# The last two layers' projections: where the second half of the rows is transposed

## The chip, the cores and the metric

The kernel runs on one core of one Trainium2 chip. The metric is the device time of one execution in microseconds (us); less is better. The kernel before took 3390.11 us in the median of three runs (3384.37 to 3390.66).

## The reference

The program is a network of four layers on 1024 tokens of width 1024, all in float32. The change touches only the last two, which `second_block` of the reference computes. Each begins in this way:

```
for l in range(DEPTH):                                  # DEPTH = 2
    shift, scale, gate = jnp.split(c_act @ ada_w[l] + ada_b[l], 3, axis=-1)
    h = rms_norm(x, norm_w[l]) * (1.0 + scale[:, None, :]) + shift[:, None, :]
    proj = h @ w_in[l]                                  # [1024, 1024] @ [1024, 2736]
```

Three mixers (a retention, a latent attention and a gated linear attention) work on `proj`, and an output product with a residual ends the layer.

## The kernel before, in words

`second_layer` calls `project` with `front=ModulatedFront(...)`. The front makes `h` in transposed form, the features on the partitions, and cuts it into two parts: `s_x_high` is the value rounded to the fast matmul type (fp32r) and `s_x_low` the rest. The weights are cut in the same manner. Each product is then three passes of eight matmuls (one for each 128 features): high weights by high rows, low weights by high rows, high weights by low rows.

The rows are 8 token tiles of 128. A half is four of them (512 tokens, one PSUM bank wide), KT = 8 is the number of 128-wide feature blocks. In `ModulatedFront` (L2767):

- `scale_rows` (L2813) multiplies a half's rows with their reciprocal root mean square, even tiles on DVE (VectorE), odd ones on ACT (ScalarE).
- `turn` (L2783) transposes on PE (TensorE): a group of four 128x128 transposes fills one bank with one feature block of one half. There are 16 groups, 64 transposes (L2792). Half 0 goes to banks 0 to 7, and half 1 goes to the same banks as half 0 leaves them.
- `modulate` on ACT (L2827) and `modulate_some` on DVE (L2833, blocks 2 and 5 of half 0) apply scale and shift and empty a bank into `s_xT`.
- `take_highs` and `leave_lows` on DVE make `s_x_high` (helper line L167) and `s_x_low` (L172).

Every engine runs its instructions in the order in which the code writes them, and semaphores tie the engines together. In `project`, `first_tiles` (L256) treats the first four jobs (token tiles 0 to 3 by the first 512 columns of weights, banks 0 to 3) together: one pass for all four (L265), then the second (L269), then the third (L273), 32 matmuls each. The later jobs come one at a time (L300, L304, L306). Job 4 writes bank 0 again, so before its first matmul PE waits until job 0 has been copied out of that bank. That copy is DVE's (`empty`, parity 0, helper line L156), and it stands in DVE's program behind everything that the front gives to DVE, `leave_lows` of half 1 the last of it.

The first of the two layers finds its first weights in SBUF already (`prefetched`). The second one loads them when the stage begins. In the rows, the first of these layers works on a tile named `x`, the second on `s_x`; both write `s_xT`, `s_x_high` and `s_x_low`.

Of the kernel before, what the change touches and what calls it, by code (L numbers as in the profile page):

```python
# [15 lines left out]
P = 128  # L16
# [169 lines left out]
def project(nc, core, chunks, slots, x, lows=None, highs=None, beside=None, front=None, ahead=0, modulation=None, prefetched=None):  # L186
# [12 lines left out]
    with stage(nc, "weights_loaded0", "weights_loaded1", "products_ready", "even_emptied", "odd_emptied",  # L199
# [35 lines left out]
        @block.tensor  # L235
        def _(pe):
            if front:
                front.turn(pe, s)
            def first_chunk():


                dst = [core.bank[n][0:jobs[n][1][1][0], 0:jobs[n][1][1][1]] for n in range(int(ends[0]))]
                parts = [[jobs[n][1][0](slot(0, w), part) for w, part in ((highs, x.high), (lows, x.high), (highs, x.low))] for n in range(int(ends[0]))]
                for k in range(KT):
                    pe.wait_ge(s["first_high"], k + 1)
                    pe.wait_ge(s["x_high"], k + 1)
                    for n in range(int(ends[0])):
                        pe.matmul(dst[n], *parts[n][0][k], start=(k == 0), stop=False)
                    pe.wait_ge(s["first_low"], k + 1)
                    pe.wait_ge(s["x_low"], k + 1)  # L250
                    for n in range(int(ends[0])):
                        pe.matmul(dst[n], *parts[n][1][k], start=False, stop=False)
                        mm = pe.matmul(dst[n], *parts[n][2][k], start=False, stop=(k == KT - 1))
                        if k == KT - 1:
                            mm.then_inc(s["products_ready"], 1)

            def first_tiles():


                firsts = [(core.bank[n][0:jobs[n][1][1][0], 0:jobs[n][1][1][1]], jobs[n][1][0]) for n in range(front.FIRST)]  # L260
                pe.wait_ge(s["w_high"], 1)
                for n, (dst, pairs) in enumerate(firsts):
                    front.ready(pe, s, n)
                    for m, (lhsT, rhs) in enumerate(pairs(slot(0, highs), x.high)):
                        pe.matmul(dst, lhsT, rhs, start=(m == 0), stop=False)  # L265
                pe.wait_ge(s["w_low"], 1)
                for dst, pairs in firsts:
                    for lhsT, rhs in pairs(slot(0, lows), x.high):
                        pe.matmul(dst, lhsT, rhs, start=False, stop=False)  # L269
                pe.wait_ge(s["x_low"], KT)  # L270
                for dst, pairs in firsts:
                    for m, (lhsT, rhs) in enumerate(pairs(slot(0, highs), x.low)):
                        mm = pe.matmul(dst, lhsT, rhs, start=False, stop=(m == KT - 1))  # L273
                    mm.then_inc(s["products_ready"], 1)

            if by_depth:
                first_chunk()
            if front:
                first_tiles()
            for n, (c, (pairs, shape, _)) in enumerate(jobs):  # L280
                if by_depth and c == 0 or front and n < front.FIRST:
                    continue
                if front:
                    front.ready(pe, s, n)
                dst = core.bank[n % banks][0:shape[0], 0:shape[1]]
                if n >= banks:

                    pe.wait_ge(emptied[(n - banks) % 2], (n - banks) // 2 + 1)
                if highs is None:
                    if n == starts[c]:  # L290
                        pe.wait_ge(loaded[c % 2], 16 * (c // 2 + 1))
                    ops = pairs(slot(c), x)
                    for m, (lhsT, rhs) in enumerate(ops):
                        mm = pe.matmul(dst, lhsT, rhs, start=(m == 0), stop=(m == len(ops) - 1))
                else:
                    if n == starts[c]:
                        pe.wait_ge(s["w_high"], c if by_depth else c + 1)
                    ops = pairs(slot(c, highs), x.high)
                    for m, (lhsT, rhs) in enumerate(ops):
                        pe.matmul(dst, lhsT, rhs, start=(m == 0), stop=False)  # L300
                    if n == starts[c]:
                        pe.wait_ge(s["w_low"], c if by_depth else c + 1)
                    for lhsT, rhs in pairs(slot(c, lows), x.high):
                        pe.matmul(dst, lhsT, rhs, start=False, stop=False)  # L304
                    for m, (lhsT, rhs) in enumerate(pairs(slot(c, highs), x.low)):
                        mm = pe.matmul(dst, lhsT, rhs, start=False, stop=(m == len(ops) - 1))  # L306
                mm.then_inc(s["products_ready"], 1)
                if modulation:
                    modulation.add_up(pe, s, n)
                if beside and beside.USES_TENSOR:  # L310
                    beside.tensor(pe, s, n)
# [17 lines left out]
        def _(dve):  # L329
# [15 lines left out]
            if front:  # L345
                front.scale_rows(dve, s, 0)
                if prefetched:
                    dve.wait_ge(loaded[0], 16)
                    take_high(dve, slot(0, highs), slot(0)).then_inc(s["w_high"], 1)
                front.scale_rows(dve, s, 1)  # L350
                front.modulate_some(dve, s)
            if by_depth:
                raw, high, low = slot(0), slot(0, highs), slot(0, lows)
                dve.wait_ge(loaded[0], 16)
                for k in range(KT):
                    take_high(dve, high[:, k, :], raw[:, k, :]).then_inc(s["first_high"], 1)
                    dve.wait_ge(s["first_high"], k + 1)
                    leave_low(dve, low[:, k, :], raw[:, k, :], high[:, k, :]).then_inc(s["first_low"], 1)
                    dve.wait_ge(s["x_high"], k + 1)
                    leave_low(dve, x.low[k], x.whole[k], x.high[k]).then_inc(s["x_low"], 1)  # L360
                split_weights(1)
            elif front:
                if not prefetched:
                    dve.wait_ge(loaded[0], 16)
                    take_high(dve, slot(0, highs), slot(0)).then_inc(s["w_high"], 1)
                front.take_highs(dve, s, 0)
                dve.wait_ge(s["w_high"], 1)
                leave_low(dve, slot(0, lows), slot(0), slot(0, highs)).then_inc(s["w_low"], 1)
                front.leave_lows(dve, s, 0)
                front.take_highs(dve, s, 1)  # L370
                front.leave_lows(dve, s, 1)
            else:
                split_weights(0)
# [2393 lines left out]
class ModulatedFront:  # L2767
# [12 lines left out]
        self.x = Halves(*[[HalfTile(halves, k) for k in range(KT)] for halves in (self.whole, self.low, self.high)])  # L2780
        self.x.split = True

    def turn(self, pe, s):  # L2783
        for n in range(2 * KT):
            half, k = divmod(n, KT)
            if k == 0:
                pe.wait_ge(s["scaled_dve"], 2 * half + 2)
                pe.wait_ge(s["scaled_act"], 2 * half + 2)
            if half:
                self.modulated(pe, s, k)  # L2790
            for i in range(4):
                mm = pe.transpose(self.core.bank[k][:, i * P:(i + 1) * P], self.rows[:, 4 * half + i, k * P:(k + 1) * P], self.core.c["ident"])  # L2792
            mm.then_inc(s["rows_turned"], 1)

    def ready(self, pe, s, n):

        if n < BANKS:
            self.modulated(pe, s, KT + n)
        if n in (0, self.FIRST):
            pe.wait_ge(s["x_high"], KT * (1 + n // self.FIRST))  # L2800
        if n == self.FIRST:
            pe.wait_ge(s["x_low"], 2 * KT)

    def modulated(self, eng, s, n):

# [12 lines left out]
            copy_out(eng, self.rows[:, t, :], self.rows[:, t, :], self.core.rstd[:, t:t + 1]).then_inc(s["scaled_act" if on_act else "scaled_dve"], 1)  # L2818

    def modulate(self, act, s):  # L2820
        self.scale_rows(act, s, 0)
        self.scale_rows(act, s, 1)
        for n in range(2 * KT):
            half, k = divmod(n, KT)
            if half or k not in self.BY_DVE:
                act.wait_ge(s["rows_turned"], n + 1)
                act.activation(self.whole[:, half, k, :], self.core.bank[k], ACT.Identity, scale=self.mod.scale[:, k:k + 1],  # L2827
                               bias=self.mod.shift[:, k:k + 1]).then_inc(s["whole_act"], 1)

    def modulate_some(self, dve, s):  # L2830
        for k in self.BY_DVE:
            dve.wait_ge(s["rows_turned"], k + 1)
            dve.tensor_scalar(self.whole[:, 0, k, :], self.core.bank[k], self.mod.scale[:, k:k + 1], self.mod.shift[:, k:k + 1],  # L2833
                              ALU.mult, ALU.add).then_inc(s["whole_dve"], 1)

    def take_highs(self, dve, s, half):
# [1250 lines left out]
```

## Time and profile before

| | us |
|---|---|
| median of three runs | 3390.11 (3384.37 to 3390.66) |
| the profiled execution | 3383.96 |
| its span in the profile | 3382.3 |
| PE busy | 3178.3 (94% of the span) |
| DVE busy | 1891.2 (56%) |
| ACT busy | 1348.8 (40%) |

The span is the profiled time from the first to the last instruction; 1.7 us of the execution lie around it. PE's records are pipelined: a matmul's record begins before that of the one ahead has ended, so the pace of a run of matmuls is read from the distance of starts, not from the duration of one. The stages of the two layers that the change touches begin at about 2170 us and 2772 us of the span. PE's granted clock is given as a share: 1.00 is its full and 0.50 its half rate.

### The profile page before, as it was taken

Reading aid. Unit: us, or ns where it says so; the run is one execution under the profiler, and the core shown is the slowest. Engines: PE = TensorE matmul, PEld = TensorE weight load, DVE = VectorE, ACT = ScalarE, POOL = GpSimd, SP = SyncE. Lnnn points to the kernel's source line nnn. Section 1 sums busy time; section 2 is a strip of 40 time slices with the busy share of each in tenths; the row PEclk is TensorE's granted clock in tenths of the full one; section 3 lists DMA queues with packets and bytes.
Section 4 is the critical chain, followed back from the end, with each engine's and each line's share of the span. In section 5 each row is a group of like instructions: output and inputs, shape, how many; then the busy total and the mean of one; then the engine's idle time right before and its main releaser. Section 6 shows DMA issues by size and latency. Waiting matters only on the chain. (4 is left out here: it accounts for less than half of the span.)

```text
span 3382.3 us, 50928 instructions
## 1 busy us (share of the span) xinstructions
PE 3178.3 (94%) x19709; PEld 2529.0 (75%) x19709; DVE 1891.2 (56%) x3524; ACT 1348.8 (40%) x2487; POOL 397.1 (12%) x313
## 2 busy tenths in 40 slices
PE   7998988899999989979799999899999989999999
PEld 6895567788876867767588888488855678896567
DVE  4535755756747644684756556634366543535654
ACT  2005851656643024552356556511344420134442
POOL 0100020334330000010024324100000000000000
PEclk9999999899999989989899999999999999999999
DMA  7517332868957410012458757610000220100012
GB/s 221 175 58 213 98 113 99 317 269 326 389 214 241 144 40 1 1 63 88 194 228 332 309 212 310 238 33 26 26 17 1 106 101 22 38 26 17 1 67 96
DMA packets 193079, 462.50 MB, mean 137 GB/s; under 512 B 44163, under 2 KB 119255, under 8 KB 184153
## 3 DMA queue, kind: packets, MB, share of 16 engines
q1 hardware_dynamic: 174425, 392.35, 32.2%
q0 software_dynamic: 18432, 67.12, 5.2%
q8 instruction: 148, 2.42, 0.3%
q14 instruction: 74, 0.61, 0.1%
HBM read 383.38 MB, written 73.33 MB: 135 GB/s over the span
## 5 line engine op out<-in xcount | busy, mean ns | idle before, releaser
L1811 PE MATMUL psum<-high_in,e_rowsT_high 128*128 128x256 f32 (+1 forms) x1080 | 330.1, 324 | 5.4 <-DVE e_rowsT_low L172 5.4
L1812 PE MATMUL psum<-high_in,e_rowsT_low 128*128 128x256 f32 (+1 forms) x1080 | 326.3, 320 | 0.0
L172 POOL TENSOR_TENSOR low_down<-w_down,high_out 128x1024 fp32r<-128x1024 f32 x64 | 209.9, 3297 | 295.0 <-ACT high_out L1889 295.0
L1811 PEld LDWEIGHTS psum<-high_in,e_rowsT_high 128*128 128x128 f32 x1080 | 206.5, 191 | 22.3 <-issue 6.1
L1812 PEld LDWEIGHTS psum<-high_in,e_rowsT_low 128*128 128x128 f32 x1080 | 206.8, 192 | 16.2
L3735 DVE CUSTOM_DVE_ANT_0 mla_probs<-psum,mla_mask 128x512 f32<-128x512 f32 (+2 forms) x192 | 97.0, 554 | 100.4 <-PE psum L3602 100.2
L172 DVE TENSOR_TENSOR low_gate<-w_gate,high_in 128x1024 fp32r<-128x1024 f32 x128 | 148.0, 1217 | 7.6 <-ACT high_in L1889 6.6
L172 DVE TENSOR_TENSOR low_up<-w_up,high_in 128x1024 fp32r<-128x1024 f32 x128 | 147.9, 1216 | 0.0
L1816 PE MATMUL psum<-low_up,e_rowsT_high 128*128 128x256 f32 x720 | 130.5, 283 | 0.0
L1889 ACT ACTIVATE high_in<-w_gate 128x1024 fp32r<-128x1024 f32 x128 | 124.8, 1058 | 6.2 <-issue 6.2
L1889 ACT ACTIVATE high_out<-w_down 128x1024 fp32r<-128x1024 f32 x128 | 124.7, 1049 | 3.8 <-DMA w_down<-in_exp_w_down 3.7
L1889 ACT ACTIVATE high_in<-w_up 128x1024 fp32r<-128x1024 f32 x128 | 124.6, 1051 | 0.0
L154 ACT ACTIVATE proj<-psum 128x512 f32<-128x512 f32 (+2 forms) x32 | 16.9, 528 | 259.0 <-PE psum L306 220.2
L156 DVE COPY proj<-psum 128x512 f32<-128x512 f32 (+2 forms) x32 | 19.3, 603 | 174.2 <-PE psum L306 173.6
L3776 ACT ACTIVATE mla_probs<-mla_probs,mla_low 128x256 f32<-128x256 f32 (+7 forms) x128 | 97.9, 767 | 46.5 <-DVE mla_low L3739 45.3
L1897 ACT ACTIVATE e_hiddenT_high<-psum 128x256 fp32r<-128x256 f32 x90 | 34.6, 385 | 204.6 <-PE psum L1825 204.6
L1835 PE MATMUL psum<-high_out,e_hiddenT_high 128*128 128x512 f32 x360 | 115.4, 402 | 0.0
L300 PE MATMUL psum<-ring_high,s_x_high 128*128 128x512 f32 (+3 forms) x576 | 112.9, 338 | 0.0
L1838 PE MATMUL psum<-low_down,e_hiddenT_high 128*128 128x512 f32 x360 | 111.8, 392 | 0.0
L1841 PE MATMUL psum<-high_out,e_hiddenT_low 128*128 128x512 f32 x360 | 111.0, 389 | 0.0
L304 PE MATMUL psum<-ring_low,s_x_high 128*128 128x512 f32 (+3 forms) x576 | 110.6, 334 | 0.0
L306 PE MATMUL psum<-ring_high,s_x_low 128*128 128x512 f32 (+3 forms) x576 | 110.6, 334 | 0.0
(604 smaller groups left out, 7586.1 us busy)
## 6 DMA issues: line engine op xcount, KB each, us to landing
w_gate<-in_exp_w_gate SPq DMA_DIRECT2D x32, 2048.0 KB, 8.8
w_up<-in_exp_w_up SPq DMA_DIRECT2D x32, 2048.0 KB, 13.6
w_down<-in_exp_w_down SPq DMA_DIRECT2D x32, 2048.0 KB, 20.1
ada<-in_ada_w SPq DMA_DIRECT2D x24, 1024.0 KB, 7.5
expert_rows<-e_out POOLq DMA_DIRECT2D x47, 512.0 KB, 7.1
expert_rows<-zero_row SPq DMA_DIRECT2D x33, 512.0 KB, 7.1
token_rows<-x SPq DMA_DIRECT2D x32, 512.0 KB, 2.6
x<-token_rows SPq DMA_DIRECT2D x24, 512.0 KB, 7.2
```

What stands on the lines that cost most here:

```text
L172: return eng.tensor_tensor(low, whole, high, ALU.subtract)
L300: pe.matmul(dst, lhsT, rhs, start=(m == 0), stop=False)
L304: pe.matmul(dst, lhsT, rhs, start=False, stop=False)
L306: mm = pe.matmul(dst, lhsT, rhs, start=False, stop=(m == len(ops) - 1))
L1811: pe.matmul(dst, rows_high[:, k, :], w_high[:, k, cols], start=(k == 0), stop=False)
L1812: pe.matmul(dst, rows_low[:, k, :], w_high[:, k, cols], start=False, stop=False)
L1816: mm = pe.matmul(dst, rows_high[:, k, :], w_low[:, k, cols], start=False, stop=(k == KT - 1))
L1835: pe.matmul(dst, hid_high[:, k, :], w_high[:, k, cols], start=(k == 0), stop=False)
L1838: pe.matmul(dst, hid_high[:, k, :], w_low[:, k, cols], start=False, stop=False)
L1841: mm = pe.matmul(dst, hid_low[:, k, :], w_high[:, k, cols], start=False, stop=(k == HT - 1))
L1889: act.activation(high(e, j)[:, k:k + STEP[j], :], W[e % 2][j][:, k:k + STEP[j], :], ACT.Copy).then_inc(s["w_high_ready"], 1)
L3776: act.activation(row, row, ACT.Exp, bias=low[:, n, side:side + 1], scale=-1.0, accum_out=sums[:, p, i // 4, side, i % 4:i % 4 + 1]).then_i ...
```

## The change

On PE, `turn` now takes a half and a range of feature blocks. Half 0 is transposed ahead, as before. Half 1 is transposed in two pieces of four groups (16 transposes each), one between the first and the second pass of the first four jobs, one between the second and the third, and both use banks 4 to 7. The first pass no longer waits until all of half 0's high parts are there: job 0's matmul m waits for high part m. Job 4 waits for half 1's high parts ahead of its first matmul and for half 1's low parts ahead of its third pass only. On ACT, the scaling of half 1's rows moves behind the modulation of half 0. On DVE, the scaling of half 1's rows moves behind half 0's `take_highs`.

```
--- before.py
+++ after.py
@@ -235,7 +235,7 @@
         @block.tensor
         def _(pe):
             if front:
-                front.turn(pe, s)
+                front.turn(pe, s, 0, range(KT))
             def first_chunk():
 
 
@@ -260,13 +260,17 @@
                 firsts = [(core.bank[n][0:jobs[n][1][1][0], 0:jobs[n][1][1][1]], jobs[n][1][0]) for n in range(front.FIRST)]
                 pe.wait_ge(s["w_high"], 1)
                 for n, (dst, pairs) in enumerate(firsts):
-                    front.ready(pe, s, n)
+                    front.modulated(pe, s, n)
                     for m, (lhsT, rhs) in enumerate(pairs(slot(0, highs), x.high)):
+                        if n == 0:
+                            pe.wait_ge(s["x_high"], m + 1)
                         pe.matmul(dst, lhsT, rhs, start=(m == 0), stop=False)
+                front.turn(pe, s, 1, range(KT // 2))
                 pe.wait_ge(s["w_low"], 1)
                 for dst, pairs in firsts:
                     for lhsT, rhs in pairs(slot(0, lows), x.high):
                         pe.matmul(dst, lhsT, rhs, start=False, stop=False)
+                front.turn(pe, s, 1, range(KT // 2, KT))
                 pe.wait_ge(s["x_low"], KT)
                 for dst, pairs in firsts:
                     for m, (lhsT, rhs) in enumerate(pairs(slot(0, highs), x.low)):
@@ -280,8 +284,8 @@
             for n, (c, (pairs, shape, _)) in enumerate(jobs):
                 if by_depth and c == 0 or front and n < front.FIRST:
                     continue
-                if front:
-                    front.ready(pe, s, n)
+                if front and n == front.FIRST:
+                    pe.wait_ge(s["x_high"], 2 * KT)
                 dst = core.bank[n % banks][0:shape[0], 0:shape[1]]
                 if n >= banks:
 
@@ -302,6 +306,8 @@
                         pe.wait_ge(s["w_low"], c if by_depth else c + 1)
                     for lhsT, rhs in pairs(slot(c, lows), x.high):
                         pe.matmul(dst, lhsT, rhs, start=False, stop=False)
+                    if front and n == front.FIRST:
+                        pe.wait_ge(s["x_low"], 2 * KT)
                     for m, (lhsT, rhs) in enumerate(pairs(slot(c, highs), x.low)):
                         mm = pe.matmul(dst, lhsT, rhs, start=False, stop=(m == len(ops) - 1))
                 mm.then_inc(s["products_ready"], 1)
@@ -347,7 +353,6 @@
                 if prefetched:
                     dve.wait_ge(loaded[0], 16)
                     take_high(dve, slot(0, highs), slot(0)).then_inc(s["w_high"], 1)
-                front.scale_rows(dve, s, 1)
                 front.modulate_some(dve, s)
             if by_depth:
                 raw, high, low = slot(0), slot(0, highs), slot(0, lows)
@@ -364,6 +369,7 @@
                     dve.wait_ge(loaded[0], 16)
                     take_high(dve, slot(0, highs), slot(0)).then_inc(s["w_high"], 1)
                 front.take_highs(dve, s, 0)
+                front.scale_rows(dve, s, 1)
                 dve.wait_ge(s["w_high"], 1)
                 leave_low(dve, slot(0, lows), slot(0), slot(0, highs)).then_inc(s["w_low"], 1)
                 front.leave_lows(dve, s, 0)
@@ -2780,26 +2786,18 @@
         self.x = Halves(*[[HalfTile(halves, k) for k in range(KT)] for halves in (self.whole, self.low, self.high)])
         self.x.split = True
 
-    def turn(self, pe, s):
-        for n in range(2 * KT):
-            half, k = divmod(n, KT)
-            if k == 0:
-                pe.wait_ge(s["scaled_dve"], 2 * half + 2)
-                pe.wait_ge(s["scaled_act"], 2 * half + 2)
+    def bank(self, half, k):
+        return self.core.bank[KT // 2 + k % (KT // 2) if half else k]
+
+    def turn(self, pe, s, half, features):
+        pe.wait_ge(s["scaled_dve"], 2 * half + 2)
+        pe.wait_ge(s["scaled_act"], 2 * half + 2)
+        for k in features:
             if half:
-                self.modulated(pe, s, k)
+                self.modulated(pe, s, KT // 2 + k)
             for i in range(4):
-                mm = pe.transpose(self.core.bank[k][:, i * P:(i + 1) * P], self.rows[:, 4 * half + i, k * P:(k + 1) * P], self.core.c["ident"])
+                mm = pe.transpose(self.bank(half, k)[:, i * P:(i + 1) * P], self.rows[:, 4 * half + i, k * P:(k + 1) * P], self.core.c["ident"])
             mm.then_inc(s["rows_turned"], 1)
-
-    def ready(self, pe, s, n):
-
-        if n < BANKS:
-            self.modulated(pe, s, KT + n)
-        if n in (0, self.FIRST):
-            pe.wait_ge(s["x_high"], KT * (1 + n // self.FIRST))
-        if n == self.FIRST:
-            pe.wait_ge(s["x_low"], 2 * KT)
 
     def modulated(self, eng, s, n):
 
@@ -2818,19 +2816,19 @@
             copy_out(eng, self.rows[:, t, :], self.rows[:, t, :], self.core.rstd[:, t:t + 1]).then_inc(s["scaled_act" if on_act else "scaled_dve"], 1)
 
     def modulate(self, act, s):
-        self.scale_rows(act, s, 0)
-        self.scale_rows(act, s, 1)
         for n in range(2 * KT):
             half, k = divmod(n, KT)
+            if k == 0:
+                self.scale_rows(act, s, half)
             if half or k not in self.BY_DVE:
                 act.wait_ge(s["rows_turned"], n + 1)
-                act.activation(self.whole[:, half, k, :], self.core.bank[k], ACT.Identity, scale=self.mod.scale[:, k:k + 1],
+                act.activation(self.whole[:, half, k, :], self.bank(half, k), ACT.Identity, scale=self.mod.scale[:, k:k + 1],
                                bias=self.mod.shift[:, k:k + 1]).then_inc(s["whole_act"], 1)
 
     def modulate_some(self, dve, s):
         for k in self.BY_DVE:
             dve.wait_ge(s["rows_turned"], k + 1)
-            dve.tensor_scalar(self.whole[:, 0, k, :], self.core.bank[k], self.mod.scale[:, k:k + 1], self.mod.shift[:, k:k + 1],
+            dve.tensor_scalar(self.whole[:, 0, k, :], self.bank(0, k), self.mod.scale[:, k:k + 1], self.mod.shift[:, k:k + 1],
                               ALU.mult, ALU.add).then_inc(s["whole_dve"], 1)
 
     def take_highs(self, dve, s, half):
```

On PE, at the start of the first of the two layers (`consts_49` is the identity matrix, `x_77` the rows), this stood before:

```order
L2792 MATMUL psum<-consts_49,x_77 128x128 x64
L265 MATMUL psum<-ring_high_25761,s_x_high_25752 128x512 x32
L269 MATMUL psum<-ring_low_25760,s_x_high_25752 128x512 x32
L273 MATMUL psum<-ring_high_25761,s_x_low_25751 128x512 x32
L300 MATMUL psum<-ring_high_25761,s_x_high_25752 128x512 x8
```

And this stands there now:

```order
L2799 MATMUL psum<-consts_49,x_77 128x128 x32
L267 MATMUL psum<-ring_high_25761,s_x_high_25752 128x512 x32
L2799 MATMUL psum<-consts_49,x_77 128x128 x16
L272 MATMUL psum<-ring_low_25760,s_x_high_25752 128x512 x32
L2799 MATMUL psum<-consts_49,x_77 128x128 x16
L277 MATMUL psum<-ring_high_25761,s_x_low_25751 128x512 x32
L304 MATMUL psum<-ring_high_25761,s_x_high_25752 128x512 x8
```

The number of transposes and of matmuls is the same; half of the transposes now stand between the passes. The second layer's order is the same.

On DVE, at the same place (`ring` is the weights, `proj` what is copied out of PSUM), this stood before:

```order
L157 TENSOR_SCALAR x_77<-x_77,rstd_56 128x1024 x2
L167 CAST ring_high_25761<-ring_19043 128x4096
L157 TENSOR_SCALAR x_77<-x_77,rstd_56 128x1024 x2
L2833 TENSOR_SCALAR s_xT_25750<-psum,mod_cols_60 128x512 x2
L167 CAST s_x_high_25752<-s_xT_25750 128x512 x8
L172 TENSOR_TENSOR ring_low_25760<-ring_19043,ring_high_25761 128x4096
L172 TENSOR_TENSOR s_x_low_25751<-s_xT_25750,s_x_high_25752 128x512 x8
L167 CAST s_x_high_25752<-s_xT_25750 128x512 x8
L172 TENSOR_TENSOR s_x_low_25751<-s_xT_25750,s_x_high_25752 128x512 x8
L156 COPY proj_321_25753<-psum 128x512
```

And this stands there now:

```order
L157 TENSOR_SCALAR x_77<-x_77,rstd_56 128x1024 x2
L167 CAST ring_high_25761<-ring_19043 128x4096
L2831 TENSOR_SCALAR s_xT_25750<-psum,mod_cols_60 128x512 x2
L167 CAST s_x_high_25752<-s_xT_25750 128x512 x8
L157 TENSOR_SCALAR x_77<-x_77,rstd_56 128x1024 x2
L172 TENSOR_TENSOR ring_low_25760<-ring_19043,ring_high_25761 128x4096
L172 TENSOR_TENSOR s_x_low_25751<-s_xT_25750,s_x_high_25752 128x512 x8
L167 CAST s_x_high_25752<-s_xT_25750 128x512 x8
L172 TENSOR_TENSOR s_x_low_25751<-s_xT_25750,s_x_high_25752 128x512 x8
L156 COPY proj_321_25753<-psum 128x512
```

Only the second pair of row scalings has moved. The last three lines are the same, but the second group of casts (half 1's high parts) waits for half 1's last transposes, which PE now makes between its passes.

## Rows read from the trace of the kernel before

**Rows 1.** The page's first line
```profile
span 3382.3 us, 50928 instructions
```

**Rows 2.** Timeline, PE, first layer's start. Start, us, engine, line, operation, [idle before <- releaser]
```profile
2172.74 9.67 PE L2792 MATMUL psum<-consts,x 128*128 128x128 f32 x64 [12.89 <-ACT x L154]
2182.17 7.51 PE L265 MATMUL psum<-ring_high,s_x_high 128*128 128x512 f32 x32
...
2196.77 7.42 PE L273 MATMUL psum<-ring_high,s_x_low 128*128 128x512 f32 x32
2204.03 1.98 PE L300 MATMUL psum<-ring_high,s_x_high 128*128 128x512 f32 x8
```

**Rows 3.** Timeline, PE, second layer's start
```profile
2775.01 8.93 PE L2792 MATMUL psum<-consts,s_x 128*128 128x128 f32 x64 [7.82 <-ACT s_x L154]
2785.80 7.53 PE L265 MATMUL psum<-ring_high,s_x_high 128*128 128x512 f32 x32 [1.86 <-DVE s_x_high L167]
...
2807.68 1.98 PE L300 MATMUL psum<-ring_high,s_x_high 128*128 128x512 f32 x8
```

**Rows 4.** Busy time of PE in the projections behind job 3, both layers
```profile
2204.00:2449.00 245.00, 244.09 (x1466) 1.00 0.10 29
2808.00:3053.00 245.00, 244.09 (x1466) 1.00 0.10 29
```

**Rows 5.** Timeline, DVE, first layer's start
```profile
2173.97 1.41 DVE L157 TENSOR_SCALAR x<-x,rstd 128x1024 f32<-128x1024 f32 x2
...
2178.09 0.81 DVE L2833 TENSOR_SCALAR s_xT<-psum,mod_cols 128x512 f32<-128x512 f32 x1 [1.71 <-PE psum L2792]
2178.96 2.77 DVE L167 CAST s_x_high<-s_xT 128x512 fp32r<-128x512 f32 x8
2181.65 4.41 DVE L172 TENSOR_TENSOR ring_low<-ring,ring_high 128x4096 fp32r<-128x4096 f32 x1
...
2193.49 4.90 DVE L172 TENSOR_TENSOR s_x_low<-s_xT,s_x_high 128x512 fp32r<-128x512 f32 x8
2198.79 0.69 DVE L156 COPY proj<-psum 128x512 f32<-128x512 f32 x1 [0.40 <-PE psum L273]
```

**Rows 6.** Timeline, DVE, second layer's start
```profile
2780.68 2.29 DVE L167 CAST ring_high<-ring 128x4096 fp32r<-128x4096 f32 x1 [0.26 <-DMA ring<-in_w_in]
2782.89 2.76 DVE L167 CAST s_x_high<-s_xT 128x512 fp32r<-128x512 f32 x8
```

**Rows 7.** Timeline, ACT, first layer's start
```profile
2170.41 4.27 ACT L154 ACTIVATE x<-x,rstd 128x1024 f32<-128x1024 f32 x4 [2.29 <-PEq L84]
...
2178.52 6.81 ACT L2827 ACTIVATE s_xT<-psum,mod_cols 128x512 f32<-128x512 f32 x10 [0.47 <-PE psum L2792]
```

**Rows 8.** Timeline, PE, transposes alone: a window at half clock, one at full clock
```profile
2172.74 4.93 PE L2792 MATMUL psum<-consts,x 128*128 128x128 f32 x22 [12.89 <-ACT x L154]
2177.67 4.63 PE L2792 MATMUL psum<-consts,x 128*128 128x128 f32 x40
```

**Rows 9.** PE by windows, second layer: window, us, busy (records), granted clock, DMA share, GB/s
```profile
2778.00:2779.00 1.00, 1.00 (x9) 0.69 1.04 403
```

**Rows 10.** Timeline, PE: first instruction behind three idle times elsewhere
```profile
361.22 0.66 PE L773 MATMUL psum<-consts,na_probs 128*128 128x128 f32 x4 [2.64 <-DVE na_probs L841]
575.54 1.72 PE L1263 MATMUL psum<-consts,x 128*128 128x128 f32 x14 [2.06 <-DVE xT L1317]
2454.11 3.43 PE L3249 MATMUL psum<-consts,proj 128*128 128x128 f32 x16 [2.31 <-PEq L84]
```

**Rows 11.** PE by windows behind those idle times: granted clock is the fourth number
```profile
362.00:363.00 1.00, 1.00 (x12) 0.50 1.05 246
365.00:366.00 1.00, 1.00 (x11) 0.81 0.74 170
576.00:577.00 1.00, 1.00 (x12) 1.00 0.90 369
2455.00:2456.00 1.00, 1.00 (x6) 0.50 0.86 83
```

More of the change, by code:

```diff
@@ L237, in _ @@
             if front:
-                front.turn(pe, s)
+                front.turn(pe, s, 0, range(KT))
             def first_chunk():
@@ L262, in first_tiles @@
                 for n, (dst, pairs) in enumerate(firsts):
-                    front.ready(pe, s, n)
+                    front.modulated(pe, s, n)
                     for m, (lhsT, rhs) in enumerate(pairs(slot(0, highs), x.high)):
+                        if n == 0:
+                            pe.wait_ge(s["x_high"], m + 1)
                         pe.matmul(dst, lhsT, rhs, start=(m == 0), stop=False)
+                front.turn(pe, s, 1, range(KT // 2))
                 pe.wait_ge(s["w_low"], 1)
@@ L269, in first_tiles @@
                         pe.matmul(dst, lhsT, rhs, start=False, stop=False)
+                front.turn(pe, s, 1, range(KT // 2, KT))
                 pe.wait_ge(s["x_low"], KT)
@@ L282, in _ @@
                     continue
-                if front:
-                    front.ready(pe, s, n)
+                if front and n == front.FIRST:
+                    pe.wait_ge(s["x_high"], 2 * KT)
                 dst = core.bank[n % banks][0:shape[0], 0:shape[1]]
@@ L304, in _ @@
                         pe.matmul(dst, lhsT, rhs, start=False, stop=False)
+                    if front and n == front.FIRST:
+                        pe.wait_ge(s["x_low"], 2 * KT)
                     for m, (lhsT, rhs) in enumerate(pairs(slot(c, highs), x.low)):
@@ L349, in _ @@
                     take_high(dve, slot(0, highs), slot(0)).then_inc(s["w_high"], 1)
-                front.scale_rows(dve, s, 1)
                 front.modulate_some(dve, s)
@@ L366, in _ @@
                 front.take_highs(dve, s, 0)
+                front.scale_rows(dve, s, 1)
                 dve.wait_ge(s["w_high"], 1)
@@ L2781, in __init__, with bank, turn @@
         self.x.split = True
[L2783 to L2788, printed above, removed]
+    def bank(self, half, k):
+        return self.core.bank[KT // 2 + k % (KT // 2) if half else k]
+    def turn(self, pe, s, half, features):
+        pe.wait_ge(s["scaled_dve"], 2 * half + 2)
+        pe.wait_ge(s["scaled_act"], 2 * half + 2)
+        for k in features:
             if half:
-                self.modulated(pe, s, k)
+                self.modulated(pe, s, KT // 2 + k)
             for i in range(4):
-                mm = pe.transpose(self.core.bank[k][:, i * P:(i + 1) * P], self.rows[:, 4 * half + i, k * P:(k + 1) * P], self.core.c["ident"])
+                mm = pe.transpose(self.bank(half, k)[:, i * P:(i + 1) * P], self.rows[:, 4 * half + i, k * P:(k + 1) * P], self.core.c["ident"])
             mm.then_inc(s["rows_turned"], 1)
[L2795 to L2802, printed above, removed]
     def modulated(self, eng, s, n):
@@ L2820, in modulate @@
     def modulate(self, act, s):
-        self.scale_rows(act, s, 0)
-        self.scale_rows(act, s, 1)
         for n in range(2 * KT):
             half, k = divmod(n, KT)
+            if k == 0:
+                self.scale_rows(act, s, half)
             if half or k not in self.BY_DVE:
                 act.wait_ge(s["rows_turned"], n + 1)
-                act.activation(self.whole[:, half, k, :], self.core.bank[k], ACT.Identity, scale=self.mod.scale[:, k:k + 1],
+                act.activation(self.whole[:, half, k, :], self.bank(half, k), ACT.Identity, scale=self.mod.scale[:, k:k + 1],
                                bias=self.mod.shift[:, k:k + 1]).then_inc(s["whole_act"], 1)
@@ L2832, in modulate_some @@
             dve.wait_ge(s["rows_turned"], k + 1)
-            dve.tensor_scalar(self.whole[:, 0, k, :], self.core.bank[k], self.mod.scale[:, k:k + 1], self.mod.shift[:, k:k + 1],
+            dve.tensor_scalar(self.whole[:, 0, k, :], self.bank(0, k), self.mod.scale[:, k:k + 1], self.mod.shift[:, k:k + 1],
                               ALU.mult, ALU.add).then_inc(s["whole_dve"], 1)
```

## The prediction

> **What bounds the kernel now.** I first read the page's span, 3382.3 us [rows 1]; the execution took 3383.96, so 1.7 us lie around it. Then the busy time of the stretches that follow the changed place. From job 4 on, PE is busy 244.09 of 245.00 us in both layers [rows 4]. So PE sets the pace of the projections behind the first four jobs, and whatever moves the start of job 4 moves all that follows by the same amount. The question is only when job 4 starts: at 2204.03 us in the first layer [rows 2] and at 2807.68 in the second [rows 3].
>
> The reader should see how tight the first layer's start already is. PE makes 64 transposes from 2172.74, goes over to the first pass at 2182.17 and runs through to job 4 without a gap [rows 2]. Nothing there waits, so a new order can only gain if it takes work off PE, and this one takes none. In the second layer PE idles once, 1.86 us ahead of the first pass, for the high parts of the rows [rows 3]. They are late because the weights land late: DVE casts the weights at 2780.68, when their transfer has arrived, and only then the rows, at 2782.89 [rows 6].
>
> **Paces.** A pass of 32 matmuls takes 2204.03 - 2196.77 = 7.26 us, 0.227 each [rows 2]. The first layer's transposes run at half clock until about 2177.67 (23 of them in 4.93 us, 0.214 each), and the other 41 take 4.50 us up to 2182.17, 0.11 each [rows 2, 8]. Sixteen at full clock cost 1.76 us. DVE's casts of the rows' blocks follow each other every (2181.65 - 2178.96)/8 = 0.336 us, and one takes 2.77 - 7 x 0.336 = 0.42 [rows 5].
>
> **First layer, step by step.** The first eight groups of transposes don't change, nor does the clock under them. ACT starts to modulate some 2.1 us sooner, since two of its four scalings (4.27/4 = 1.07 us each) move behind it [rows 7]. But DVE casts in order, and ahead of its first cast stands its own block 5, which waits for the sixth group of transposes until 2178.09 and ends at 2178.90 [rows 5]. So the first cast stays at 2178.96: "modulated sooner" buys nothing here.
>
> What changes is that PE need not wait for 64 transposes. Its first matmul starts when the first cast has ended, 2178.96 + 0.42 + 0.05 = 2179.43. Job 0's eight matmuls come at the casts' pace (7 x 0.336 = 2.35), and the other 24 and the slot of the last at 0.227 (25 x 0.227 = 5.68), so the first pass ends at 2187.46. Before it ended at 2182.17 + 7.26 = 2189.43: 2.0 us gained. Then 1.76 us of transposes (2189.22), the second pass (2196.48), 1.76 again (2198.24), and the third pass to 2205.50. PE by itself is now 1.5 us later than 2204.03. The two pieces of transposes (3.5 us) used to stand ahead of the first pass, and only 2.0 us of them are covered by starting sooner: the rest is the idle time while DVE makes the first high part (0.7 us) and the slower eight matmuls.
>
> The second pass needs the low weights. DVE's row scaling (1.41) and the low weights (4.41) follow the casts: 2181.65 + 1.4 + 4.4 = 2187.5, before 2189.22 [rows 5]. No wait. ACT's modulations of half 1 are spread over two pieces and come at 0.67 us each (6.81/10) [rows 7], faster than DVE needs them. A cost of changing between the two kinds of matmul isn't seen at 2182.17, where one follows the other without a gap [rows 2]; the second run is 0.09 us longer than the third (7.51 against 7.42). Four more changes in a layer cost between 0 and 0.4 us; I take 0.
>
> Now DVE's queue, which decides. Half 1's casts wait for the last transposes, which PE now makes at 2198.24 and which DVE sees some 0.2 us later. Then come eight casts (2.69), eight low parts (4.90), and only behind them the copy of job 0 out of bank 0 (0.69) [rows 5]. That is 2198.44 + 2.69 + 4.90 + 0.69 = 2206.72. Job 4 writes that bank, so it starts at 2206.7, not at 2205.5. Before, DVE had ended its low parts at 2198.39 and idled 0.40 us for job 0 [rows 5]: a wait that didn't exist takes the place. First layer: +2.7 us.
>
> **Second layer.** The first cast stays at 2782.89, since the weights' transfer sets it [rows 6]. First matmul 2783.36, end of the first pass 8.03 later at 2791.39 (before 2793.06), then 1.76, 7.26, 1.76: last transposes at 2802.17, third pass over at 2809.43. DVE: 2802.37 + 2.69 + 4.90 + 0.69 = 2810.65, against 2807.68 before: +3.0 us. Here the half 1 transposes had been wholly hidden behind the weights' transfer, and now they aren't.
>
> **The clock in the second layer.** PE's clock rises at about 2778.62 (0.69 over that microsecond) [rows 9]. So 3.6 us at 0.214 are 17 transposes, the other 15 of half 0 end at 2780.3, and PE then idles until 2783.36, 3.0 us, where it idled 1.86. Elsewhere idle times of 2.64 and 2.31 us were followed by half clock, one of 2.06 was not [rows 10, 11]. So I take it that the clock falls. The low spell behind the 2.64 us gap is over during the microsecond from 365, some 3.4 us after 362 [rows 11]. At half clock a matmul takes 2 x 0.227 = 0.45. In 3.4 us PE then does 7.5 of them; at full clock it would do the eight paced ones in 2.4 us and four more in the last 1.0. That is about 4.7 matmuls, 1.1 us. The ends are 0 (no fall) and 3.4 us (two such spells, all of it on unpaced work). I take 1.1.
> The Trainium skill ("TensorE: Matmul & The Clock Gate", "Why this matters for your kernels") asks for no idle gaps above about 3 us between bursts. By that rule the new gap is just at the limit and the fall could stay away, which is the second case below; this case's trace is stricter, with falls behind 2.31 and 2.64 us.
>
> **Sum.** 2.7 + 3.0 + 1.1 = 6.8 us. On the profiled execution that is 3383.96 + 6.8 = 3390.8; on the median 3390.11 + 6.8 = 3396.9. The four times of before lie in two groups (3384.0 and 3384.4, 3390.1 and 3390.7), so the new median may be drawn from either. I say 3396.
>
> **Rivals.**
> - *The clock holds.* Then +5.7 us, 3395.8. For it: the 2.06 us gap that held; against it: 3.0 us is longer than two gaps that didn't.
> - *A long low spell.* The clock stays low over two spells: 5.7 + 3.4 = 9.1 us, 3399.2. For it: the first eight matmuls are spaced at 0.336 us, sparser than any pass of before, and could keep the clock low. Against it: the low spell behind the 2.64 us gap ended within 4 us [rows 11].
> - *The copy isn't waited for.* If the low parts of half 1 overlapped the third pass more than I count, only PE's own 1.5 + 1.8 us would remain: +3.3 us, 3393.4. Against it: DVE's 8.3 us of queue behind the last transpose are longer than the third pass's 7.26.
> - *Not slower: the transposes between the passes are free.* If PE took them in beside the matmuls of the passes (their weights load while a matmul runs), the last transposes and DVE's queue move up by 3.5 us in each layer, to 2203.2 and 2807.1 at job 4: -0.8 and -0.5, together -1.3 us, 3388.8. It would decide at any price below 0.02 us a transpose. Against it: 0.11 us a transpose with PE busy throughout [rows 8], and I see no reason why that should change between passes.
>
> **Chances.** Forecast 0.50, clock holds 0.25, long spell 0.10, copy not waited for 0.07, free transposes 0.08. A difference of 0.2% (6.8 us) is about what a measurement of this kernel can tell from none, and the forecast lies on that line. From the cases and the 6 us between the two groups of times: slower by more 0.44, within 0.50, faster 0.06. The range, 3387 to 3402, takes in the free transposes and the long spell, with two or three us of scatter.
>
> **What the new profile would show.** Right: first pass at about 2179.4 and 2783.4; in each layer two pieces of 16 transposes of 1.8 us each with no idle time before them; DVE's copy of job 0 directly behind the low parts; PE idle ahead of job 4 for about 1.2 us, released by that copy; job 4 at 2206.7 and, counted from its stage's start, 3.0 us later in the second layer, more if the clock falls. Wrong: a first cast clearly before 2178.96, transposes at less than 0.1 us, no idle time ahead of job 4, or half clock during the first layer's passes. If DVE or the weights delayed the second pass, that would be a step I have costed at nothing.

## The result, and the profile after

The changed kernel takes 3397.53 us in the median of ten runs (3390.37 to 3403.04), the kernel before 3388.36 in the same comparison (3382.67 to 3392.18). The ratio is 1.003 with a 95% interval of 1.0021 to 1.0040: slower by 7 to 14 us, the lower end just above the 0.2% (6.8 us) that the prediction set as its bound.

The profiled execution took 3390.37 us, of which the page's first line shows this span, 6.4 us above that of before [rows 1]:

```profile
span 3388.7 us, 50922 instructions
```

PE's timeline at the first layer's start, to be laid beside [rows 2] (start, us, engine, line, operation, and in brackets the idle time before it and what ended it):

```profile
2171.95 5.69 PE L2799 MATMUL psum<-consts,x 128*128 128x128 f32 x32 [12.88 <-ACT x L154]
2178.24 8.22 PE L267 MATMUL psum<-ring_high,s_x_high 128*128 128x512 f32 x32 [0.61 <-DVE s_x_high L167]
2186.31 1.91 PE L2799 MATMUL psum<-consts,x 128*128 128x128 f32 x16
2187.97 7.51 PE L272 MATMUL psum<-ring_low,s_x_high 128*128 128x512 f32 x32
2195.33 1.91 PE L2799 MATMUL psum<-consts,x 128*128 128x128 f32 x16
2196.99 7.54 PE L277 MATMUL psum<-ring_high,s_x_low 128*128 128x512 f32 x32
2205.61 2.09 PE L304 MATMUL psum<-ring_high,s_x_high 128*128 128x512 f32 x8 [1.08 <-DVE proj L156]
```

The reader should see three things that [rows 2] didn't have: 0.61 us of idle time ahead of the first pass, two pieces of 16 transposes (1.66 us each, from a piece's start to the start of the pass behind it), and 1.08 us of idle time ahead of job 4 that ended with DVE's copy of job 0. Job 4 starts 33.66 us behind the first transpose, where it was 31.29. Part of this pair's distance is the clock, which rose about 1 us sooner behind the first transpose than before (PE by windows: window, us, busy, then the granted clock; first the kernel before, whose transposes begin at 2172.74, then the changed one, at 2171.95):

```profile
2177.00:2178.00 1.00, 1.00 (x8) 0.57 1.03 312
2176.00:2177.00 1.00, 1.00 (x11) 0.97 1.01 362
```

DVE's timeline there, to be laid beside [rows 5]:

```profile
2176.80 0.81 DVE L2831 TENSOR_SCALAR s_xT<-psum,mod_cols 128x512 f32<-128x512 f32 x1 [1.21 <-PE psum L2799]
2177.67 2.77 DVE L167 CAST s_x_high<-s_xT 128x512 fp32r<-128x512 f32 x8
...
2197.27 2.77 DVE L167 CAST s_x_high<-s_xT 128x512 fp32r<-128x512 f32 x8 [6.35 <-PE psum L2799]
2199.97 4.90 DVE L172 TENSOR_TENSOR s_x_low<-s_xT,s_x_high 128x512 fp32r<-128x512 f32 x8
2204.78 0.68 DVE L156 COPY proj<-psum 128x512 f32<-128x512 f32 x1
```

DVE's first cast still stands directly behind its own block 5. Then, new, DVE idles 6.35 us for the last transposes, and its casts, low parts and copy run on end to end behind them. They finish after PE has run out of work. The casts can't begin with the blocks that are ready: `s_x_high` lies in SBUF where the rows lie (both are placed at `AT_X`), so `take_highs` waits until all eight groups of its half are transposed. That is why the second piece, and not the first, sets when DVE's 8.3 us of casts, low parts and copy begin.

PE's timeline at the second layer's start, beside [rows 3]:

```profile
2776.85 5.32 PE L2799 MATMUL psum<-consts,s_x 128*128 128x128 f32 x32 [7.82 <-ACT s_x L154]
2785.24 9.67 PE L267 MATMUL psum<-ring_high,s_x_high 128*128 128x512 f32 x32 [3.07 <-DVE s_x_high L167]
2794.75 1.91 PE L2799 MATMUL psum<-consts,s_x 128*128 128x128 f32 x16
...
2814.06 2.09 PE L304 MATMUL psum<-ring_high,s_x_high 128*128 128x512 f32 x8 [1.08 <-DVE proj L156]
```

The idle time ahead of the first pass is 3.07 us where it was 1.86, and the pass takes 1.45 us longer than the first layer's. PE by windows shows why:

```profile
2784.00:2785.00 1.00, 0.00 (x0) 1.00 0.90 268
2786.00:2787.00 1.00, 1.00 (x4) 1.00 1.05 387
2788.00:2789.00 1.00, 1.00 (x3) 0.50 1.04 397
2790.00:2791.00 1.00, 1.00 (x5) 0.77 0.22 22
```

The clock falls behind the idle time, in the first pass, and is back at full some 3.4 us later (0.50, then 0.77 in the microsecond from 2790). Job 4 starts 37.21 us behind the first transpose instead of 32.67. Behind job 4 PE's work is what it was in [rows 4]:

```profile
2206.00:2451.00 245.00, 244.09 (x1466) 1.00 0.10 29
2815.00:3060.00 245.00, 244.09 (x1466) 1.00 0.10 29
```

So the two starts cost 2.37 + 4.54 = 6.9 us in this pair of profiles; the spans differ by 6.4.

### The profile page after: what moved, and what is told of

It is laid out like the page before. It is cut to its first block and busy times, and to the rows that moved or that the text cites. A ratio compares the mean times of both kernels' runs of the same rounds, so it can differ in the third digit from the quotient of the medians.

```text
span 3388.7 us, 50922 instructions
## 1 busy us (share of the span) xinstructions
PE 3179.2 (94%) x19709; PEld 2526.8 (75%) x19709; DVE 1891.5 (56%) x3524; ACT 1349.6 (40%) x2487; POOL 397.2 (12%) x313
```

## The experiments

"To job 4" is the time from the stage's first transpose to job 4's first matmul. Medians, ratios and intervals are against the kernel before in the same rounds.

**first_only and second_only.** The changed order in one layer alone. `ModulatedFront` got a switch, and both orders stand in the code behind it:

```
-    front = ModulatedFront(core, x, mod)
+    front = ModulatedFront(core, x, mod, (True, False)[l], (True, False)[l])   # first_only; (False, True) in second_only
...
+                if not front.interleaved:
+                    front.turn(pe, s, 1, range(KT))
```

> The changed order in the first of the two layers only; the second layer's start is the kernel before's. Theory (every term sits in its own layer, and later work shifts with job 4): from the first transpose to job 4 33.7 us in the first layer, 32.7 in the second, span 2.4 us above the kernel before. Rival (part of the loss comes from the clock in later stages and not from the two starts): the time stays 4 us or more above the kernel before although the second start is as before.

> The changed order in the second of the two layers only. Theory: 31.3 us from the first transpose to job 4 in the first layer, 37.2 in the second (3.0 us for the copy and the uncovered transposes, 1.5 for the low clock in the first pass), span 4.5 us above the kernel before. Rival (the low clock in the first pass was a chance of the one profiled run): no low clock there and 3.0 us instead of 4.5.

Measured: first_only 34.30 us and 32.68 us to job 4, second_only 31.37 and 37.17. Each layer's cost sits in its own start. (34.30 is 0.6 above what was expected: in this profile the clock rose later under the transposes.) PE's timeline of second_only at its second layer has the changed kernel's low-clock pass again:

```profile
2783.20 9.55 PE L269 MATMUL psum<-ring_high,s_x_high 128*128 128x512 f32 x32 [3.28 <-DVE s_x_high L167]
```

The ratios are 1.001 (0.9995 to 1.0025) and 1.0005 (0.999 to 1.002). Neither half by itself can be told from no change. The median of first_only is 4.9 us above the kernel before, as the rival on other stages had it, but its interval reaches from -2 to 8 us, so the times neither show that rival nor exclude it. The spans don't tell either: first_only's is 7.1 us above that of before, with 577.72 us between job 4 and the second layer's first transpose where the kernel before had 570.98 (below, changed_again_2).

**copy_early.** DVE's copy of job 0 goes ahead of half 1's low parts:

```
                 front.take_highs(dve, s, 1)
+                empty(dve, 0, 0, 1)
                 front.leave_lows(dve, s, 1)
...
-                empty(dve, 0, int(starts[c]), middle)
+                empty(dve, 0, int(starts[c]) + (1 if front and c == 0 else 0), middle)
```

> The changed kernel, with DVE's copy of job 0 moved ahead of half 1's low parts. Theory (job 4 waits for DVE's queue): PE's idle time ahead of job 4, 1.08 us in each layer, is gone, job 4 starts 1.1 us sooner in each, span 2.2 us under the changed kernel. Rival (the low parts, now 0.7 us later, are missed by job 4's third pass): the idle time moves there and nothing is gained.

PE's timeline, first the first layer's last pass and job 4, then the second layer's two passes at either end and job 4:

```profile
2196.19 7.51 PE L277 MATMUL psum<-ring_high,s_x_low 128*128 128x512 f32 x32
2203.54 1.98 PE L304 MATMUL psum<-ring_high,s_x_high 128*128 128x512 f32 x8
...
2790.92 8.23 PE L267 MATMUL psum<-ring_high,s_x_high 128*128 128x512 f32 x32 [2.66 <-DVE s_x_high L167]
...
2809.70 7.51 PE L277 MATMUL psum<-ring_high,s_x_low 128*128 128x512 f32 x32
2817.05 1.98 PE L304 MATMUL psum<-ring_high,s_x_high 128*128 128x512 f32 x8
```

The idle time ahead of job 4 is gone in both layers, and none appears at the third pass of job 4. From the first pass to job 4 it is 26.13 us instead of 27.37: 1.2 us a layer, as the wait's 1.08 said. The ratio is 1.0023 (1.0008 to 1.0039); the span went up to 3391.6, not down by 2.2, because of stages that the edit doesn't touch (578.92 us between the starts). The copy's wait is shown; its worth in time is only read from the profile. The kernel as changed did not run in the same rounds, so no time shows the gain. One thing I hadn't expected: with an idle time of 2.66 us the clock did not fall here (8.23 us for the pass).

**filled.** Work for PE in the second layer's idle time:

```
                 front.turn(pe, s, 0, range(KT))
+                if not prefetched:
+                    front.modulated(pe, s, 4)
+                    for i in range(20):
+                        pe.transpose(core.bank[4][:, 0:P], core.c["ident"], core.c["ident"])
```

> The changed kernel, with 20 transposes of the identity put into the second layer's idle time ahead of the first pass (bank 4, overwritten later; their results are not used). Theory (the idle time of 3.1 us brings the clock down): the idle time falls to about 0.9 us, the clock stays at 1.00 through the first pass, which takes 8.2 us instead of 9.7, and job 4 starts 1.4 us sooner, though PE does more. Rival (the sparse first eight matmuls bring the clock down, not the idle time): the clock falls in the first pass as before and the 20 transposes gain nothing.

PE's timeline at its second layer:

```profile
2785.11 5.20 PE L2803 MATMUL psum<-consts,s_x 128*128 128x128 f32 x32 [7.82 <-ACT s_x L154]
2790.14 2.36 PE L242 MATMUL psum<-consts 128*128 128x128 f32 x20
2793.64 8.23 PE L271 MATMUL psum<-ring_high,s_x_high 128*128 128x512 f32 x32 [1.14 <-DVE s_x_high L167]
...
2821.04 1.16 PE L308 MATMUL psum<-ring_high,s_x_high 128*128 128x512 f32 x4 [1.11 <-DVE proj L156]
```

With 1.14 us of idle time the pass takes 8.23 us, and job 4 comes at 35.93 us, 1.3 sooner than in the changed kernel, though PE made 20 more transposes. The first eight matmuls are as sparse as before, so by themselves they don't bring the clock down; each_wait_2 and half_early below have them too, at full clock. It is one profile, and copy_early's clock held without any filling, so the run shows what a pass without the fall costs (1.3 to 1.4 us less than in the changed kernel's first profile) and not that filling always prevents it. The ratio is 1.0015 (1.000 to 1.003).

**each_wait_2.** The kernel before with the finer wait of job 0 alone:

```
-                    front.ready(pe, s, n)
+                    front.modulated(pe, s, KT + n)
                     for m, (lhsT, rhs) in enumerate(pairs(slot(0, highs), x.high)):
+                        if n == 0:
+                            pe.wait_ge(s["x_high"], m + 1)
```

> The kernel before, with one part of the change alone: job 0's matmul m waits for high part m instead of all eight. All 64 transposes stay ahead of the first pass. Theory (the transposes belong into the second layer's wait for its weights): first layer unchanged (31.3 us from the first transpose to job 4), second layer's first pass starts right behind the last transpose, and job 4 comes 30.9 us behind the first transpose instead of 32.7, a gain of 1.7 us. Rival (the sparse first matmuls bring the clock down): no gain, and half clock in that pass.

PE's timeline at its second layer:

```profile
2788.85 8.66 PE L2794 MATMUL psum<-consts,s_x 128*128 128x128 f32 x64 [7.82 <-ACT s_x L154]
2797.26 8.24 PE L267 MATMUL psum<-ring_high,s_x_high 128*128 128x512 f32 x32
...
2819.85 1.98 PE L302 MATMUL psum<-ring_high,s_x_high 128*128 128x512 f32 x8
```

31.00 us to job 4 instead of 32.67, no idle time ahead of the pass and no low clock; the first layer is as before (30.88). The time is 3391.65 us against 3394.65, a ratio of 0.9989 (0.9978 to 1.0000). The gain of 1.7 us is seen in the profile and fits the ratio, but is below 0.2%.

**changed_again_2 and before_again_2.** Both kernels once more, without an edit.

> The changed kernel once more, in the same rounds as the kernel before. Theory (the two starts cost 6.9 us, the clock's falls in other stages scatter and add nothing on the average): 33.1 to 34.3 us and 35.7 to 37.2 us from the first transpose to job 4, and a ratio between 1.001 and 1.003. Rival (the changed order costs some 3 us more elsewhere): a ratio of 1.003 again, and a stage behind the two starts that is longer in this profile too.

> The kernel before against itself, for its scatter. Theory: a ratio of 1.000 with an interval of about 0.0015 to each side, 31.3 to 31.9 us and 32.7 us from the first transpose to job 4. Its profile shows whether low clock in the attention stage of the first layer (2510 to 2680 us) comes without the change too.

The changed kernel took 3403.91 us, the kernel before 3394.65, 9.3 us between the medians; the ratio is 1.0023 (1.0015 to 1.0032), 5 to 11 us. The kernel before against itself gave 0.9997 (0.9988 to 1.0006). To job 4: 32.96 and 36.57 us in the changed kernel; 30.38 and 32.68 in the kernel before. The changed kernel's clock fell in the second layer's first pass again (PE's timeline and one window):

```profile
2801.24 8.87 PE L267 MATMUL psum<-ring_high,s_x_high 128*128 128x512 f32 x32 [2.66 <-DVE s_x_high L167]
```
```profile
2802.00:2803.00 1.00, 1.00 (x4) 0.50 1.03 389
```

The rest of the span scatters in both orders. From job 4 of the first layer to the first transpose of the second it was 571 us in five profiles (before, after, second_only, half_early: 570.96 to 571.50; filled 571.71) and 574 to 580 in the six others, 579.40 of the kernel before among them. The difference goes with one idle time in the attention stage. PE idles 2.00 us there in every profile, and behind it the clock holds in some and falls in others. The kernel before has it both ways in its first layer, first the profile in which the clock holds, then the one in which it falls:

```profile
2512.45 0.49 PE L3598 MATMUL psum<-mla_knT,mla_qnT 64*128 64x128 f32 x4 [2.00 <-PEq L84]
2518.27 0.65 PE L3598 MATMUL psum<-mla_knT,mla_qnT 64*128 64x128 f32 x4 [2.00 <-PEq L84]
```

The windows of the second one (the 2.00 us end at 2518.27):

```profile
2517.00:2518.00 1.00, 0.00 (x0) 1.00 0.00 0
2518.00:2519.00 1.00, 0.73 (x6) 0.74 0.00 0
2520.00:2521.00 1.00, 1.00 (x6) 0.50 0.00 0
2524.00:2525.00 1.00, 1.00 (x4) 0.50 0.00 0
```

The second layer has the same idle time. Where the clock held behind it, the stretch from job 4 to the span's end took 569.7 to 570.1 us (three profiles), where it fell 574.6 to 578.9 (eight). In both layers every long stretch has the fall and no short one has it. Nor is the stretch ahead of the change steady: the first transpose comes at 2167.7 to 2183.5 us, although the code ahead of it is the same. So single spans say nothing about 2 us here.

Does the fall come more often with the changed order? In the eleven profiles (two layers each) it came in 10 of the 12 layers with the changed order, copy_early's, filled's and double_turn's among them, and in 4 of the 10 others, half_early's two among these. That can still be chance. No run was made to settle it.

**half_early.** Each piece of half 1's transposes one place earlier. The scaling of half 1's rows also goes back to where it stood in the kernel before, on DVE and on ACT (left out of the lines shown):

```
+                front.turn(pe, s, 1, range(KT // 2))
                 pe.wait_ge(s["w_high"], 1)
...
-                front.turn(pe, s, 1, range(KT // 2))
+                front.turn(pe, s, 1, range(KT // 2, KT))
                 pe.wait_ge(s["w_low"], 1)
...
-                front.turn(pe, s, 1, range(KT // 2, KT))
                 pe.wait_ge(s["x_low"], KT)
```

> The changed kernel with each piece of half 1's transposes one place earlier: the first ahead of the first pass, the second between the first and the second pass, none between the second and the third; the row scalings stand where they stood in the kernel before. Theory (what costs is that PE idles or crawls while transposes are left to do, and that DVE sees the last of them late): PE's idle time ahead of the second layer's first pass about 1.3 us, no low clock there, no idle time ahead of job 4, and job 4 level with the kernel before: 30.1 to 31.3 us and 32.7 us behind the first transpose. Rival (any transposes between passes cost more than their own 1.7 us): job 4 later than in the kernel before by 1 us or more.

PE's timeline at its second layer:

```profile
2782.11 7.03 PE L2799 MATMUL psum<-consts,s_x 128*128 128x128 f32 x48 [7.82 <-ACT s_x L154]
2790.54 8.22 PE L268 MATMUL psum<-ring_high,s_x_high 128*128 128x512 f32 x32 [1.40 <-ACT s_xT L2826]
2798.61 1.91 PE L2799 MATMUL psum<-consts,s_x 128*128 128x128 f32 x16
...
2814.87 1.98 PE L304 MATMUL psum<-ring_high,s_x_high 128*128 128x512 f32 x8
```

30.96 and 32.76 us to job 4: level with the kernel before, although 16 transposes still stand between passes. DVE sees the last of them one pass sooner, and the idle time ahead of job 4 is gone. The time agrees, with a ratio of 1.0001 (0.9990 to 1.0012).

**double_turn.** Every transpose of half 1 twice, one execution:

```
-            for i in range(4):
+            for i in (range(4) if not half else [0, 1, 2, 3, 0, 1, 2, 3]):
```

> The changed kernel with every transpose of half 1 done twice, 32 more in each layer; the values are the same. Theory (a transpose between passes costs PE its 0.104 us): each piece takes 3.3 us instead of 1.66, and job 4 starts 3.3 us later in each layer than in the changed kernel, copy wait still 1.1 us. Rival (they are free beside the matmuls' passes): less than 1 us later.

PE's timeline at its first layer:

```profile
2174.13 8.21 PE L267 MATMUL psum<-ring_high,s_x_high 128*128 128x512 f32 x32 [0.61 <-DVE s_x_high L167]
2182.18 3.65 PE L2799 MATMUL psum<-consts,x 128*128 128x128 f32 x32
2185.59 7.52 PE L272 MATMUL psum<-ring_low,s_x_high 128*128 128x512 f32 x32
...
2204.98 2.08 PE L304 MATMUL psum<-ring_high,s_x_high 128*128 128x512 f32 x8 [1.08 <-DVE proj L156]
```

A piece takes 3.41 us instead of 1.66, and from the first pass to job 4 it is 30.85 us instead of 27.37: 3.5 us for 32 transposes, 0.109 each. They aren't free. In the second layer the first pass has the low clock again (8.87 us behind 2.66 us of idle time).

## Why the prediction was right

The time forecast was 3396, measured 3397.53. The closeness of the two is in part luck: the forecast starts from a median of 3390.11, 1.75 us above that of the later ten runs, and the loss itself was 9.2 us between the medians where 6.8 was forecast. By its own steps:

- *PE sets the pace behind job 4.* Right: 244.09 of 245.00 us busy again, and each layer's cost appears alone in first_only and second_only.
- *The first cast stays, "modulated sooner" buys nothing.* Right: it follows block 5 directly, at 2176.80 and 2177.67. Counted from the first transpose it came 5.72 us later where it had been 6.22, and block 5 was sooner by the same 0.50: that is the clock's earlier rise under the transposes, not ACT's start.
- *PE by itself 1.5 us later in the first layer.* The idle time was foretold as 0.7 us (measured 0.61), the first pass as 8.03 us (8.07), a piece of transposes as 1.76 (1.66). The four further changes between the kinds of matmul were costed at nothing; the second pass, which stands behind a piece, takes 7.36 us, 0.1 longer than 7.26, and the cheaper transposes give that back. Two hand-overs were set without a row: 0.05 us from DVE's first cast to PE's first matmul, where [rows 3, 6] have 0.15 (2782.89 + 2.76 to 2785.80), and 0.2 us from the last transpose to DVE's casts, which the profile after has as 0.28 (2196.99 to 2197.27).
- *DVE's queue decides job 4.* Right: idle time of 1.08 us where 1.2 was forecast, ended by that copy; copy_early takes it away.
- *First layer +2.7 us.* The one pair of profiles gave 2.37, with the clock's earlier rise in the profile after. Over more profiles: the old order took 31.29, 30.38, 30.88 (each_wait_2) and 31.37 us to job 4 (mean 30.98), the changed one 33.66, 34.30, 33.95 (filled, whose first layer is the changed one's) and 32.96 (mean 33.72). That is +2.7.
- *Second layer +3.0, and the clock +1.1.* Old order 32.67, 32.68 and 32.68; changed 37.21, 37.17 and 36.57 (mean 36.98): +4.3. The longer first pass is 1.4, 1.3 and 0.65 us of it, 1.1 in the mean, as the term for the clock had it; the rest is 3.2 where 3.0 was forecast. And the fall isn't certain: it came in four of the five profiles that kept the gap (double_turn's pass took 8.70 us), and copy_early's held. So the rival "the clock holds" comes true in some executions.
- *The transposes between passes aren't free.* double_turn shows it, at 0.109 us each.

The sum from these means is 7.0 us, against the 6.8 of the forecast. Both measured intervals hold or nearly hold it: 5 to 11 us in changed_again_2 and 7 to 14 us in the first comparison. Both differences of medians are 9.2 and 9.3 us, though, and what lies beyond 7 is open. The fall behind the 2.00 us idle time in the attention stage goes with a stretch some 3 to 9 us longer. If it does come more often with the changed order, it could account for what lies beyond 7, and the prediction has no term for it.

The chances put "within 0.2%" a little above "slower"; the ratios are 1.0030 and 1.0023, the intervals start at 1.0021 and 1.0015. Neither interval reaches 1, so the loss is clear, and it lies at or a little above that bound, as the forecast did.

No run beat the kernel before clearly. The best is each_wait_2, which keeps the one part of the change that helps: the 64 transposes stay where the second layer waits for its weights anyway, and the first pass starts with the first high part. Its gain is 1.7 us in the second layer's start; the interval of its time ends at 1.0000.

## What to carry to other kernels

Work that PE does while it would wait anyway costs nothing, as half of the transposes did in the second layer; moving it behind that wait to start the next thing sooner puts it on the path. Before an order is changed, look at what the second engine has queued behind the moved work: here DVE needed 8.3 us behind the last transpose, and PE had 7.3 us of work to cover it. An engine with slack over the whole span (DVE is busy 56% of it) can still be the one that is late at one place. And a finer wait may be worth taking alone, out of a change whose other parts lose.

## What the runs showed of the hardware

The length of an idle time does not settle by itself whether the granted clock falls from 1.00 to 0.50 behind it. With 2.66 us ahead of the same pass it held once (8.23 us for the pass, copy_early) and fell twice (8.87 us both times, changed_again_2 and double_turn). Behind 3.07 and 3.28 us it fell both times (9.67 and 9.55 us). The 2.00 us of the attention stage come twice in each of the eleven profiles, and behind them the clock fell in 14 of the 22 cases.

The fall can come in the work behind the idle time: in the changed kernel's second layer PE starts again at 2785.24 with 1.00, and the clock falls to 0.50 about 1.8 us later (0.52 in the microsecond from 2787).

Transposes alone bring the clock back from 0.50 to 1.00. At the first layer's start PE does nothing else, and the clock rose 5.1 us behind the first transpose in the kernel before and about 4 us behind it in the changed one.
